# Expert stage with a weight ring of eight slots, scaled down products and the last sums behind the overflow jump

## The chip, the cores and the metric

The kernel runs on one core of a Trainium2 chip. The metric is the device time of one execution in microseconds (us). The engines are named as in the profile: PE is TensorE (PEld its weight loads), DVE is VectorE, ACT is ScalarE, POOL is GpSimd, SP is SyncE, which here only issues weight transfers.

## The reference

Two transformer blocks on 256 tokens of width 1024, all in float32. The first ends in a mixture of 32 experts, each token going to four of them; the second begins with a norm of the result. What matters here:

```python
def _moe(h, ...):
    logits = h @ router_w + router_b
    top_logit, top_e = lax.top_k(logits, 4)
    top_w = softmax(top_logit)
    ...
        gate = minimum(xe @ w_gate[e] + b_gate[e], 7.0)
        up = clip(xe @ w_up[e] + b_up[e], -7.0, 7.0)
        act = (up + 1) * (gate * sigmoid(1.702 * gate))
        return act @ w_down[e] + b_down[e]
    ...
    y = yb[dest] * sorted_w[:, None]
    return segment_sum(y, sorted_tok, num_segments=t)

# first block, end
x = x + g_m * moe(modulate(rmsnorm(x, norm_mlp), sh_m, sc_m))
# second block, start
h = rmsnorm(x, norm_mix_2); proj = h @ w_in_2
```

## The kernel before, in words

All weights stream through one ring of six slots (`RING`) of 2.097 MB; SP issues one transfer per block, in the order of use, each after a wait that TensorE has freed a block (`block_used`). The experts need 192 blocks: two halves each of w_gate, w_up and w_down for 32 experts, in eight groups of four (`EG`). Seven groups run in a hardware loop (`Fori`), the eighth is written out behind it. `expert_load` (L374) issues them; TensorE multiplies a half in `halves` (L1629), each 128x64 tokens by 512 columns.

A group on TensorE (`group_pe`): for each expert the gate product, the transpose of the previous expert's activation (L1651), the up product, then the previous expert's down product. In it lie the gather of the next group's tokens (L1617), the transpose of the slot weights (L1660), and two `combine` steps (L1677), which multiply the down results of a pair of experts by those slot weights, back to token order. VectorE adds the gate bias (L1115), clips (L1117), multiplies by the sigmoid (L1123), adds the up bias (L1125), and forms the activation (L1129); it fetches the next bias row by a shuffle (L1106). ScalarE makes the sigmoid (L638), and copies the down product from PSUM to `ypair` in two copies (`y_out`, L651 and L652). VectorE adds each of the four results of a combine from PSUM to the accumulator `acc` (L1141); two PSUM banks take them in turn, so a result waits until the one two before it has been read.

The down biases are multiplied by the token weights on TensorE at the start (L1718) and copied to `acc` by ScalarE (L685).

A token slot table holds 64 tokens per expert. If an expert has more, further passes run. The code of those passes is written out behind the first pass on every engine (`ov_passes`: a value is loaded, and a branch passes over it if it is 1). With these inputs the branch is always taken: 64 loads of w_gate are seen, those of one pass. After it VectorE multiplies `acc` by `g_moe` (L1188) and adds it to the residual `xres` (L1190), for each of two tiles of 128 tokens. ScalarE sums the squares of a tile (L606), VectorE forms the mean (L831), GpSimd the inverse root (L431), VectorE scales the tile (L1018), TensorE transposes it (L1573), ScalarE (L705) and VectorE (L1196) take the transposed halves out of PSUM. Then the projections of the second block begin (L1364, the helper of all ordinary products). GpSimd clears three tiles `Q2` for them (L447) as soon as `xres` is complete; ScalarE writes into the first of them from its first projection (L729).

Before the stage, the attention branches are merged (VectorE, `merged_done`, L1012), then come the output products (W_OUT, two blocks), the norm, the router products and the ranking on VectorE (L1050 to L1091). The arena area from column 13312 on holds `sig` and `prob`, last read before the merge ends.

## Time and profile before

| | us |
|---|---|
| median of 3 runs | 1884.38 (1884.05 to 1886.4) |
| the profiled execution | 1884.26 |
| its span, first to last instruction | 1882.5 |
| PE busy (share of the span) | 1706.3 (91%) |
| DVE busy | 454.0 (24%) |
| ACT busy | 306.4 (16%) |
| expert blocks issued, w_gate, w_up, w_down | 64 each, 2048 KB a block |

The profile is of one execution. Its page gives busy times and 40 slices of the span, 47 us each. The table of stretches gives the same for stretches one chooses, with the clock granted to TensorE as a share of 2.4 GHz, the mean share of the sixteen DMA engines, and GB/s. The chain of waits follows the work that ended last backwards, from each step to what released it. The list in order of time shows instructions merged into runs (x is their number). "issue" marks time in which an engine waited for nothing that the profile shows. A busy PE also counts the pipeline's filling.

### The profile page before, as it was taken

Reading aid. Unit: us, or ns where it says so; the run is one execution under the profiler, and the core shown is the slowest. Engines: PE = TensorE matmul, PEld = TensorE weight load, DVE = VectorE, ACT = ScalarE, POOL = GpSimd, SP = SyncE. Lnnn points to the kernel's source line nnn. Section 1 sums busy time; section 2 is a strip of 40 time slices with the busy share of each in tenths; the row PEclk is TensorE's granted clock in tenths of the full one; section 3 lists DMA queues with packets and bytes.
Section 4 is the critical chain, followed back from the end, with each engine's and each line's share of the span. In section 5 each row is a group of like instructions: output and inputs, shape, how many; then the busy total and the mean of one; then the engine's idle time right before and its main releaser. Section 6 shows DMA issues by size and latency. Waiting matters only on the chain.

```text
span 1882.5 us, 18274 instructions
## 1 busy us (share of the span) xinstructions
PE 1706.3 (91%) x7238; PEld 901.1 (48%) x7238; DVE 454.0 (24%) x928; ACT 306.4 (16%) x620; POOL 29.2 (2%) x30
## 2 busy tenths in 40 slices
PE   4999999899989898898988989875999999999998
PEld 1545686533233232332323323222767788588643
DVE  1342432232222222222222222224022221211001
ACT  2122450311010110110101101001242222000000
POOL 0110000000000000000000000001000000000000
PEclk9999999899999999999999999997999999989999
DMA  9776223499999999999999999998323233334410
GB/s 369 281 258 192 90 95 119 170 430 428 428 428 428 429 429 429 428 428 429 429 428 428 429 429 428 428 427 330 123 101 134 90 135 134 134 135 148 165 45 23
DMA packets 86888, 537.01 MB, mean 285 GB/s; under 512 B 4624, under 2 KB 5776, under 8 KB 62256
## 3 DMA queue, kind: packets, MB, share of 16 engines
q1 hardware_dynamic: 84736, 530.60, 69.7%
q10 hardware_dynamic: 2096, 5.64, 0.8%
q8 instruction: 38, 0.62, 0.1%
q14 instruction: 18, 0.15, 0.0%
HBM read 535.17 MB, written 1.05 MB: 285 GB/s over the span
## 4 chain that ended last, share of the span: by engine, by line
PE 73%; DMA 21%; DVE 3%; issue 2%; ACT 1%; SPq 1%; DVEq 0%; POOL 0%; POOLq 0%; ACTq 0%
PE ps L1364 33%; PE ps L1629 22%; DMA ring<-in_w_up 17%; PE ps L1925 5%; PE ps L1617 3%; PE ps L1677 3%; DMA ring<-in_w_down 3%; DMA ring<-in_w_ada 1%; PE ps L1377 1%; PE ps L1518 1%; PE ps L1651 1%; SPq L339 1%; DVE arena L1106 0%; PE ps L1470 0%; DVE arena L1018 0%
## 5 line engine op out<-in xcount | busy, mean ns | idle before, releaser
L1629 PE MATMUL ps<-ring,arena 128*64 128x512 f32 x3072 | 687.6, 598 | 79.7 <-DMA ring<-in_w_gate 33.3
L1629 PEld LDWEIGHTS ps<-ring,arena 128*64 128x64 f32 x3072 | 218.4, 137 | 524.6 <-issue 429.7
L1364 PE MATMUL ps<-arena,ring 128*128 128x256 f32 x1856 | 414.5, 383 | 2.8 <-ACT arena L705 2.5
L1364 PEld LDWEIGHTS ps<-arena,ring 128*128 128x128 f32 x1856 | 354.3, 192 | 62.8 <-issue 7.1
L1364 PE MATMUL ps<-ring,arena 128*128 128x512 f32 (+1 forms) x480 | 197.1, 566 | 4.6 <-issue 3.4
L1364 PEld LDWEIGHTS ps<-ring,arena 128*128 128x128 f32 x480 | 89.7, 190 | 103.6 <-issue 99.6
L1115 DVE TENSOR_TENSOR arena<-ps,arena 128x512 f32<-128x512 f32 x32 | 22.1, 692 | 383.5 <-PE ps L1629 383.5
L1925 PE MATMUL ps<-ring,arena 128*128 128x512 f32 x256 | 110.0, 592 | 0.0
L1677 PE MATMUL ps<-arena 128*128 128x512 f32 x128 | 68.2, 664 | 21.7 <-DVE arena L1141 20.4
L1125 DVE TENSOR_TENSOR arena<-ps,arena 128x512 f32<-128x512 f32 x32 | 22.1, 692 | 249.7 <-PE ps L1629 249.7
L1925 PEld LDWEIGHTS ps<-ring,arena 128*128 128x128 f32 x256 | 48.6, 190 | 60.8 <-issue 60.7
L643 ACT ACTIVATE arena<-ps 128x512 f32<-128x512 f32 x32 | 19.1, 597 | 347.7 <-PE ps L1651 347.7
L651 ACT ACTIVATE arena<-ps 64x512 f32<-64x512 f32 x32 | 18.9, 590 | 307.5 <-PE ps L1629 307.5
L1617 PE MATMUL ps<-arena 128*128 128x256 f32 x256 | 59.6, 393 | 3.9 <-DVE arena L1098 3.9
L1617 PEld LDWEIGHTS ps<-arena 128*128 128x128 f32 x256 | 49.6, 196 | 16.6 <-issue 5.7
L1141 DVE TENSOR_TENSOR arena<-ps,arena 128x512 f32<-128x512 f32 x64 | 43.6, 690 | 36.6 <-PE ps L1677 35.6
L431 POOL TENSOR_TENSOR stat<-stat 128x8 f32<-128x8 f32 (+3 forms) x22 | 23.6, 1074 | 1848.3 <-DVE stat L831 1848.3
L1377 PE MATMUL ps<-ring,router_weights 128*32 128x512 f32 x192 | 28.1, 710 | 25.6 <-DMA const<-in_const 17.3
L1677 PEld LDWEIGHTS ps<-arena 128*128 128x128 f32 x128 | 22.3, 200 | 58.3 <-DVE arena L1141 40.6
L606 ACT ACTIVATE arena<-xres 128x1024 f32<-128x1024 f32 x8 | 8.5, 1057 | 217.9 <-DVE xres L1336 109.4
L1106 DVE STREAM_SHUFFLE arena<-arena 128x1024 f32<-128x1024 f32 x33 | 42.9, 1299 | 0.3
L1329 DVE TENSOR_TENSOR arena<-arena 128x512 f32<-128x512 f32 x16 | 11.1, 692 | 104.1 <-ACT arena L821 104.1
(229 smaller groups left out, 915.0 us busy)
## 6 DMA issues: line engine op xcount, KB each, us to landing
ring<-in_w_up SPq DMA_DIRECT2D x72, 2048.0 KB, 21.3
ring<-in_w_down SPq DMA_DIRECT2D x72, 2048.0 KB, 25.5
ring<-in_w_gate SPq DMA_DIRECT2D x64, 2048.0 KB, 24.1
ring<-in_w_in SPq DMA_DIRECT2D x23, 2048.0 KB, 8.0
ring<-in_w_ada SPq DMA_DIRECT2D x12, 2048.0 KB, 16.0
ring<-in_w_out SPq DMA_DIRECT2D x4, 2048.0 KB, 7.8
ring<-in_w_branch SPq DMA_DIRECT2D x3, 2048.0 KB, 7.7
ring<-in_w_oa SPq DMA_DIRECT2D x2, 1024.0 KB, 11.6
```

What stands on the lines that cost most here:

```text
L431: pool.tensor_tensor(a, a, stat[:, 240:240 + a.shape[1]], ALU.pow).then_inc(sem("root_done"), 1)
L643: act.activation(actT, bank(3).rearrange("p (c f s) -> p c f s", c=4, f=2), ACT.Copy).then_inc(X["tr_read"], 1)
L1106: dve.stream_shuffle(bias, btab, [q] * 32)
L1115: dve.tensor_tensor(gbuf, bank(0), bias[:, 0:512], ALU.add).then_inc(X["gate_read"], 1)
L1125: dve.tensor_tensor(ubuf, bank(1), bias[:, 512:1024], ALU.add).then_inc(X["up_read"], 1)
L1141: dve.tensor_tensor(a, bank(6 + r % 2), a, ALU.add).then_inc(X["comb_read"], 1)
L1364: last = pe.matmul(dst, a, b, start=k == 0, stop=k == len(terms) - 1)
L1377: last = pe.matmul(bank(ada_bank(n))[32 * g:32 * g + 32, :], cs_t[:, 2 * g + c, :], w[:, 2 * g + c, :], start=c == 0, stop=c == 1)
L1617: last = pe.matmul(bank(4 + r % 2)[:, T * jj:T * jj + T], hperm[:, tt, j // 4, j % 4, :], S4[:, tt].rearrange("p e s -> p (e s)"), start=t ...
L1629: mm = pe.matmul(dst[CAP * g:CAP * g + CAP, :], stationary(half, c), w[:, c, 512 * g:512 * g + 512], start=half == 0 and c == 0, stop=half ...
L1677: pe.matmul(bank(6 + r % 2), WST[:, P * (2 * pr + tt):P * (2 * pr + tt) + P], ypair[:, pr, 512 * h:512 * h + 512], start=True, stop=True). ...
L1925: last = pe.matmul(bank(4 + 2 * tt + hh), hid[:, 4 * i + c, P * tt:P * tt + P], w[:, c, 512 * hh:512 * hh + 512], start=i == 0 and c == 0, ...
```

## The change

- Expert blocks go through eight slots: position k modulo 8 = 4 and 5 lie in the arena from column 13312 (two slots of 4096 columns), the others in the six of the ring. Each load now waits for the block eight before it (`MRING`). The first four expert blocks wait as before; the loads behind them wait besides for `merged_done`.
- The expert tiles in the arena move together to make room; `acc` goes away.
- The down products are taken out of PSUM by VectorE, multiplied by `g_moe` in the same instruction. The results of the combine steps are added straight into `xres`. The down biases are scaled by `g_moe` before their product, and the four results added to `xres` by VectorE.
- In the last group, the last down product's multiplication and the last four sums stand behind the overflow branch on VectorE (`finish`). The last combine on TensorE, ahead of its branch, writes to four banks and waits once, for the four sums of the combine before.
- GpSimd clears `Q2` after both tiles are scaled (`hx_xn`), no longer after the residual is complete.
- The second block's loads count on semaphores of their own; the first six take their slots from the last expert blocks.

```diff
+        def moe_ring(k):
+            s = k % MRING
+            return None if s in (4, 5) else (W_MOE + (s if s < 4 else s - 2)) % RING
+        def moe_block(k):
+            s = moe_ring(k)
+            a = ring[:, s * SLOT:(s + 1) * SLOT] if s is not None else area(13312 + SLOT * (k % MRING - 4), SLOT)
...
             with e.If(n > 1):
-                if before:
-                    before()
                 with e.Fori(1, n) as p:
+                    if before:
+                        before(p)
...
+                j = i - W_QKV2
+                if j >= RING:
+                    sp_.wait_ge(used2, j - RING + 1)
+                elif j >= 0:
+                    sp_.wait_ge(block_used, passes[0] * (GROUPS * GROUP_BLOCKS) + (W_MOE - MRING + (j if j < 4 else j + 2) + 1))
...
-                    sp_.wait_ge(X["used"], u * GROUP_BLOCKS + (X["before"] - RING + k + half + 1))
+                        sp_.wait_ge(X["used"], u * GROUP_BLOCKS + (X["before"] - MRING + k + half + 1))
...
+                expert_load(X, u0, 0, 0, 0, free=W_MOE - RING + 1 if first else None)
+                expert_load(X, u0, 0, 0, 1, free=W_MOE - RING + 3 if first else None)
+                if first:
+                    sp_.wait_ge(sem("merged_done"), 4)
...
-            pool.wait_ge(sem("x2_done"), 2)
+            pool.wait_ge(sem("hx_xn"), 2)
...
-            def y_out(X, u, q, last=False):
-                act.activation(y[r0:r0 + CAP, 0:512], bank(2)[0:CAP, :], ACT.Copy)
-                act.activation(y[r0:r0 + CAP, 512:1024], bank(2)[CAP:2 * CAP, :],
-                               ACT.Copy).then_inc(X["y_read"], 1)
+            def y_out(X, u, q, last=False):
+                dve.tensor_tensor(y[r0:r0 + CAP, 0:512], bank(2)[0:CAP, :], g_moe[0:CAP, 0:512], ALU.mult)
+                dve.tensor_tensor(y[r0:r0 + CAP, 512:1024], bank(2)[CAP:2 * CAP, :], g_moe[CAP:2 * CAP, 512:1024],
+                                  ALU.mult).then_inc(X["y_read"], 1)
...
+            def finish(X, it, u, final):
+                y_out(X, u, EG - 1, True)
+                for r in range(4):
+                    tt, h = r // 2, r % 2
+                    dve.wait_ge(X["comb_done"], it * 8 + (8 + r + 1))
+                    xx = xres[:, tt, 512 * h:512 * h + 512]
+                    add = dve.tensor_tensor(xx, bank((6, 7, 4, 5)[r]), xx, ALU.add)
+                    add.then_inc(sem("x2_done") if final else X["comb_read"], 1)
...
                 for q in range(1, EG):
                     gate_dve(X, u, q)
                     up_dve(X, it, u, q)
+                    y_out(X, u, q - 1)
                 if not last:
                     gate_dve(X, u, EG)
                 combine_dve(X, it, 0)
                 if not last:
+                    y_out(X, u, EG - 1)
                     up_dve(X, it, u, EG)
-                combine_dve(X, it, 1)
+                    combine_dve(X, it, 1)
...
+                if first:
+                    dve.tensor_tensor(bdown[0:N_EXP, :], bdown[0:N_EXP, :], g_moe[0:N_EXP, :],
+                                      ALU.mult).then_inc(sem("bd_read"), 1)
...
-            dve.drain()
-            for i in range(TT):
-                dve.tensor_tensor(acc[:, i, :], acc[:, i, :], g_moe[:, :], ALU.mult)
-                dve.drain()
-                dve.tensor_tensor(xres[:, i, :], xres[:, i, :], acc[:, i, :], ALU.add).then_inc(sem("x2_done"), 1)
+            n = ov_passes(dve, more_dve, lambda p: finish(X, p * GROUPS - 1, p * GROUPS - 1, False))
+            finish(X, n * GROUPS - 1, n * GROUPS - 1, True)
...
-            def combine(X, it, pr):
+            def combine(X, it, pr, last=False):
+                if last:
+                    pe.wait_ge(X["comb_read"], it * 8 + 5)
...
-                    pe.matmul(bank(6 + r % 2), WST[:, P * (2 * pr + tt):P * (2 * pr + tt) + P],
+                    pe.matmul(bank((6, 7, 4, 5)[r] if last else 6 + r % 2),
+                              WST[:, P * (2 * pr + tt):P * (2 * pr + tt) + P],
```

## Rows read from the trace of the kernel before

**Rows 1.** The page: part 2 (DMA share in tenths, 40 slices), part 4 by line.

```profile
DMA  9776223499999999999999999998323233334410
PE ps L1364 33%; PE ps L1629 22%; DMA ring<-in_w_up 17%; PE ps L1925 5%; PE ps L1617 3%; PE ps L1677 3%; DMA ring<-in_w_down 3%; DMA ring<-in_w_ada 1%; PE ps L1377 1%; PE ps L1518 1%; PE ps L1651 1%; SPq L339 1%; DVE arena L1106 0%; PE ps L1470 0%; DVE arena L1018 0%
```

**Rows 2.** Table of stretches, around and in the expert stage; columns in its first row.

```profile
core 0: us, PE busy (x) PEld busy (x) DVE busy (x) ACT busy (x) POOL busy (x), PEclk, DMA share, GB/s
310.00:325.00 15.00, 15.00 (x42) 7.08 (x41) 4.87 (x9) 2.22 (x6) 0.55 (x1) 1.00 0.02 7
340.00:360.00 20.00, 15.47 (x61) 12.37 (x62) 5.29 (x26) 7.38 (x11) 0.00 (x0) 0.67 0.00 0
412.00:1277.00 865.00, 765.38 (x3320) 279.57 (x3320) 218.03 (x339) 93.18 (x155) 0.00 (x0) 0.99 1.01 428
1277.00:1310.00 33.00, 13.80 (x52) 6.13 (x48) 15.17 (x16) 5.42 (x14) 6.33 (x5) 0.73 1.04 383
```

**Rows 3.** In order of time, SP's issues: start, length to the last one's end.

```profile
287.57 16.49 SPq L374 DMA_DIRECT2D ring<-in_w_up  x2
325.39 6.46 SPq L374 DMA_DIRECT2D ring<-in_w_gate  x2
362.48 3.77 SPq L374 DMA_DIRECT2D ring<-in_w_up  x2
```

**Rows 4.** The waits of TensorE: total us, times, longest.

```profile
PE ps L1629 <- DMA ring<-in_w_gate: 33.3, 29, 1.3
```

**Rows 5.** Groups of instructions in the stage: busy, mean ns, idle before.

```profile
L651 ACT ACTIVATE arena<-ps 64x512 f32<-64x512 f32 x32 | 18.9, 590 | 307.5 <-PE ps L1629 307.5
L1115 DVE TENSOR_TENSOR arena<-ps,arena 128x512 f32<-128x512 f32 x32 | 22.1, 692 | 383.5 <-PE ps L1629 383.5
```

**Rows 6.** The chain that ended last, 1262 to 1312 us: start, us, what.

```profile
1268.10 3.65 PE ps L1629 x16
...
1275.97 7.04 PE ps L1629 x32
...
1284.28 3.91 PE ps L1677 x8
...
1289.20 5.68 issue
...
1302.30 5.70 DVE arena L1018
...
1308.05 1.13 PE ps L1573 x4
```

**Rows 7.** In order of time, 1262 to 1312 us: start, us, engine, line, idle before.

```profile
1276.01 0.69 DVE L1141 TENSOR_TENSOR arena<-ps,arena 128x512 f32<-128x512 f32 x1 [0.17 <-PE ps L1677]
...
1284.30 0.38 ACTq L699 DMA_DIRECT2D g_attn<-in_norm_final  x1
...
1285.44 0.69 DVE L1141 TENSOR_TENSOR arena<-ps,arena 128x512 f32<-128x512 f32 x1 [8.74 <-PE ps L1677]
...
1299.89 0.15 DVE L831 TENSOR_SCALAR stat<-stat 128x1 f32<-128x1 f32 x1
...
1301.57 1.97 PE L1573 MATMUL ps<-const,arena 128*128 128x128 f32 x8 [13.40 <-DVE arena L1018]
...
1302.15 5.30 POOL L447 MEMSET arena<- 128x2048 f32 x3
...
1311.28 16.28 PE L1364 MATMUL ps<-arena,ring 128*128 128x256 f32 x64 [1.26 <-ACT arena L705]
```

**Rows 8.** DMA queues: instruction packets, MB, share: 1291 to 1292, then 1292 to 1293.

```profile
q8 instruction: 1, 0.02, 6.8%
...
q14 instruction: 1, 0.01, 2.5%
```

**Rows 9.** Table of stretches, around TensorE's idle time; columns as in rows 2.

```profile
1290.00:1295.00 5.00, 0.00 (x0) 0.00 (x0) 0.00 (x0) 0.00 (x0) 0.00 (x0) 0.69 1.05 385
1315.00:1320.00 5.00, 5.00 (x23) 4.32 (x22) 0.00 (x0) 0.00 (x0) 0.00 (x0) 0.92 0.00 0
```

More of the change, by code:

```diff
@@ L277, in two_blocks, with moe_loaded, moe_loads_before @@
         loaded = [sem(f"block_loaded{s}") for s in range(RING)]
-        X1 = {n: sem("x_" + n) for n in (
+        X = {n: sem("x_" + n) for n in (
             "gate_read", "gate_min", "up_read", "sig_done", "act_done", "tr_done", "tr_read", "y_read",
             "comb_done", "comb_read", "s4_ready", "ws4_ready", "gather_done", "gather_read")}
-        X2 = dict(X1)
-        X1["used"], X1["loaded"], X1["before"], X1["slot"] = block_used, loaded, W_MOE, W_MOE
-        X2["used"] = sem("more_block_used")
-        X2["loaded"] = [sem(f"more_block_loaded{i}") for i in range(RING)]
-        X2["before"], X2["slot"] = RING, 0
+        X["used"], X["before"] = block_used, W_MOE
+        MRING = 8
+        def moe_ring(k):
[4 more added lines that the diff above has]
+            a = ring[:, s * SLOT:(s + 1) * SLOT] if s is not None else area(13312 + SLOT * (k % MRING - 4), SLOT)
+            return a.rearrange("p (c n) -> p c n", c=4)
+        def moe_loaded(k):
+            s = moe_ring(k)
+            return sem(f"extra_loaded{k % MRING - 4}") if s is None else loaded[s]
+        def moe_loads_before(k):
+            s = moe_ring(k)
+            return 0 if s is None else len(range(s, W_MOE, RING))
+        loaded2 = [sem(f"block2_loaded{s}") for s in range(RING)]
+        used2 = sem("block2_used")
         block = ctx.enter_context(nc.Block())
@@ L1357, in tell_used @@
                 if owed[0]:
-                    first.then_inc(block_used, 1)
+                    first.then_inc(used_now[0], 1)
                 owed[0] = False
@@ L1623, in halves @@
                 for half in range(2):
-                    i = X["slot"] + weight_block(q, m, last) + half
-                    pe.wait_ge(X["loaded"][i % RING], u * (16 * GROUP_BLOCKS // RING) + 16 * (i // RING + 1))
-                    w = w4_view(i)
+                    b = weight_block(q, m, last) + half
+                    pe.wait_ge(moe_loaded(b), u * (16 * GROUP_BLOCKS // MRING) + 16 * (moe_loads_before(b) + b // MRING + 1))
+                    w = moe_block(b)
                     for c in range(4):
@@ L1703, in group_pe @@
                     up(X, it, u, EG)
-                combine(X, it, 1)
+                combine(X, it, 1, last)
             def slot_bias_transpose():
@@ L1931, in _ @@
                 if i < 7:
-                    last.then_inc(block_used, 1)
+                    last.then_inc(used2, 1)
 def launch_arrays(inp):
```

147 lines of the change are left out of this document (74 added, 73 removed).

## The prediction

> **What bounds the kernel now.** I read the chain that ended last first, by line [rows 1]. A third of it is ordinary TensorE work in the attention parts and the second block (L1364), nearly all the rest is the expert stage: matmuls of L1629 and waits for the transfers of w_up and w_down. Then the table of stretches [rows 2]. In the expert stage, 412 to 1277 us, the sixteen DMA engines are busy the whole time (share 1.01, 428 GB/s) while TensorE is busy for 765 of 865 us: the stage is bound by its weight transfers, 192 blocks of 2.097 MB. Such a block takes 2.097 MB / 428 GB/s = 4.90 us. TensorE's own waits for weights are short and many (29 waits for w_gate, 33.3 us) [rows 4]: it uses every block as it lands, with the ring nearly empty. Before the stage the same engines stand still: share 0.02 in 310 to 325, 0.00 in 340 to 360 [rows 2]. The issue queue shows why [rows 3]: six blocks are out at 331.9 us (two w_gate at 325.39, the second some 6 us later), and the seventh needs a slot that TensorE frees only at 362.48. Last, the end of the stage, step by step [rows 6, 7]: after the last down product (ends 1283.0) there are 28.25 us to the first projection of the next block (1311.28), in which TensorE does little. In them stand a gap of 5.68 us on VectorE in which no visible thing is waited for, at the place where it jumps over the code of the overflow passes, and a normalisation of 5.70 us for tile 1, where the same instruction took 0.75 us for tile 0.
>
> **Ring of eight.** The blocks of group positions 4 and 5 of every eight go to two arena slots. The wait of the first two (merged_done 4 and the 22nd and 23rd freed block) is over when the pair of [rows 3] at 287.57 has gone out (304.1), because merged_done is counted by VectorE before the output products begin. They move in 304 to 325, where the engines stand nearly still. The two after them take the issue times of today's blocks 4 and 5, 325.39 and about 331.5, and land before 340. So at 362.48 eight blocks are there, not six. Nothing later is issued at another condition: each transfer still waits for a block that TensorE frees, and until 412 TensorE runs without a wait for weights, so it frees them at today's times. From then on the engines are busy throughout, so the landing of block n depends on how many blocks are still to move: two fewer, 2 x 4.90 = 9.8 us earlier. Lower bound of this gain: 0 (if something else paces the stage); upper bound 9.8. I take 9.8, since the share is 1.01 from 412 to 1277 and 1.04 from there to 1310 [rows 2]. The last down product waits for the second half of down product 2 (TensorE restarts on it at 1268.10), not for its own blocks, so its end moves with the transfers from 1283.0 to 1273.2.
>
> **Down products read by VectorE.** Two copies of 0.59 us on ScalarE per expert (L651, its twin L652) become two multiplications on VectorE. The nearest row is the 128x512 sum with one PSUM operand, 0.69 us (L1115) [rows 5]: 1.45 us with gaps, 32 times, 46 us more VectorE work spread over 915 us. It hides behind TensorE's products of 7.1 us per matrix: the 32 instructions of L1115 alone waited 383.5 us for TensorE [rows 5]. Behind the waiting multiplication VectorE has the next gate sum (TensorE waits for that one two products later), whose product ends 7 us after the down product. If that cover were gone, TensorE would lengthen by at most 46 us, and it has 100 us of idle time in [rows 2]. Price 0. The same holds for the scaling of the down biases (32 partitions, once, before TensorE's first gate product ends) and for the four bias sums that go from ScalarE to VectorE (4 x 0.69 us, before the up product of expert 0 ends).
>
> **The end of the stage.** I count from the end of the last down product. Today: 1.25 us for the two ScalarE copies, 3.9 us of combine (starts 1284.28), VectorE's last sum, the gap, two multiplications and two sums over 128x1024, the normalisation, 28.25 in all.
> Changed: VectorE makes its jump after the first four sums of the last group, not after the last four. Those end at 1276.70 today (the last starts at 1276.01 [rows 7]), 6.3 us before the down product ends. The jump costs 5.68 plus some 0.4 us around it, so it is just covered. Then 1.5 us (two multiplications) to the combine, which needs no sums in between as it has four banks, 3.9 us, ends at 5.4. The sums into the residual start 1.16 us after each result (1284.28 to 1285.44) and are paced by it at 0.86: the last ends at 5.95. ScalarE squares tile 0 from 4.2, tile 1 from 6.0. From the mean (L831, 1299.89) to TensorE's transpose (1301.57) are 1.7 us [rows 7]: tile 0 is ready at 7.7, tile 1, 1.5 us behind, at 9.2. The scaled products make the two multiplications and the separate sums (4 x 1.2 us) fall away.
> Now what is late next. TensorE also has the overflow code to skip, and it makes its jump after the combine, at 5.4. Today that is hidden behind 13.4 us of idling. Its price has no row of its own, but the instruction queues have two: a packet of 16 KB at 1291 to 1292 (q8) and one of 8 KB at 1292 to 1293 (q14) [rows 8], both during VectorE's gap, and VectorE goes on at 1294.9. So two engines fetch, and one is TensorE (the queue with the larger packets: no other engine has nearly as long a program to pass over). Its packet comes 3.4 us after its combine ends, VectorE's 3.7 us after its gap begins. Bounds: 0, as on ScalarE, which issues its next transfer at 1284.30, 0.07 us after its last copy [rows 7]; and 13.4, the idle time that covers it. I take VectorE's 5.7. TensorE then starts at 11.1, 1.9 us after tile 1 is ready, does the eight transposes of tile 0 in 1.97, and the projections start 3.2 us after the second eight begin (1308.05 to 1311.28): 11.1 + 2.0 + 3.2 = 16.3 us instead of 28.25. Gain 12.0.
> The Trainium skill, "Runtime: NRT & Kernel Launch", section Instruction fetch mechanics, says that a taken branch whose target lies outside the pages held forces a fetch before execution goes on; it speaks against leaving TensorE's jump where it is. The two packets agree. By it alone TensorE waits and the gain of this part is 12.0; were the jump free, 15.3.
>
> **Later clearing.** GpSimd's three memsets (1302.15, 5.30 us) and tile 1's normalisation (1302.30, 5.70 us) begin and end together [rows 6, 7]: the normalisation waited them out. They now start when both tiles are done, at 9.2, and end at 14.6. ScalarE first needs the cleared tile some 9.4 us after the projections start, at 25. The 4.9 us are inside the 12.0 above. Unknown is whether VectorE's reads of transposed tiles (from PSUM) are held as well: no row. If they are, those of tile 0, due at 13.1, wait until 14.6, and the projections move by 0.7 at most; bounds 0 and 0.7, I take 0.
> On this the Trainium skill, "GPSIMD Engine Reference", section Specifications, says that GpSimd's SBUF interface is contended by Vector instructions in a two-port mode or with two SBUF inputs. The reads in question have one input, in PSUM; by it the price is 0, by the held row 0.7.
>
> **TensorE's clock.** It fell to its lower level (1.2 GHz) in 1290 to 1295, after TensorE had stood still since 1288.2, and was back at the upper (2.4 GHz) within 1315 to 1320, mean 0.92 [rows 9], so about 4.5 us into the projections; half of that, 2.3 us, was lost. The idle stretch is now 5.7 us, so I let it fall again and take 0, with a gain of 2.3 as bound.
>
> **Sum.** 9.8 + 12.0 = 21.8 us. All after 1311 is one dense TensorE chain that moves as a whole: its transfers take at most four tenths of the engines [rows 1]. Four of its blocks can be issued before the last down product, the others right behind. Span 1882.5 - 21.8 = 1860.7; the profiled execution took 1884.26, 1.8 us more than its span, and stands 0.1 under the median of 1884.38. Forecast 1862.5.
>
> **Rivals.**
> TensorE's jump is hidden: it may prefetch further than VectorE. Then the transposes start at 7.7, the projections at 12.9, gain 9.8 + 15.3 = 25.1: 1859.2. For it: ScalarE's free jump. Against: the 16 KB packet after the jump. 0.13.
> VectorE's jump is no longer covered: 6.1 us stand against 6.3, and the fetch now queues behind 16 KB pieces of expert weights. At twice 5.7 the multiplications start 5.5 us late and everything behind them: 1868.0; at half of that surcharge 1865. 0.14.
> The lead of two blocks is lost, by a stage that TensorE or a queue paces: only the 12.0 stay, 1872.3. Against: share 1.01. 0.06.
> Slower: the arena slots. 48 of the 192 blocks now land beside the buffers that the engines write. The other level of the engines in this trace is 383 GB/s (1277 to 1310, share 1.04, columns of the next matrices) [rows 2], 5.48 us a block. Were it theirs in these slots, 48 x 0.58 = 28 us are lost: 1862.5 + 28 = 1890. It decides from 0.45 us a block, 21.8 / 48. Against: the rate held 428 on average while all four engines worked in the arena. 0.03.
>
> **How the numbers follow.** The forecast with its own spread of 2 us (clock, memset) has 0.62; the rest, 0.02, is an effect below what can be told. The range 1857.5 to 1868 takes the forecast, the hidden jump with the clock's gain and the uncovered jump, and leaves out the lost lead and the arena: 0.87 to 0.89. A change within 0.2%, 3.8 us, is about what a measurement of this kernel can't tell from none. Faster 0.95 (0.62 + 0.13 + 0.14 + 0.06), same 0.02, slower 0.03.
>
> **What would show it.** Two transfers right behind 303.7; eight out before 340; the landing of the last expert block 9.8 us earlier. On VectorE a gap of about 6 us between the fourth and the multiplication of the last down product. On TensorE a gap of 5 to 6 us after the last combine while normalised tiles lie ready. The normalisation of tile 1 at 0.75 us. Wrong I would be with a DMA share under 1 in the stage, or a first multiplication that begins well after the last down product ended.

## The result and the profile after

| | before | changed |
|---|---|---|
| median, us | 1884.81 (4 runs) | 1858.54 (4 runs, 1857.39 to 1859.68) |
| ratio | | 0.9855, interval 0.9842 to 0.9868 |
| the profiled execution, its span | 1884.26, 1882.5 | 1857.39, 1855.0 |

By the ratio the change takes 27.3 us off (0.9855 of 1884.4 is 1857.1); the two medians of the table lie 26.3 apart, the two spans 27.5. The forecast was 21.8, with a range of 1857.5 to 1868, so the time by the ratio lies just below the range. Line numbers shift: `halves` is now L1669, the combine L1720, the ordinary products L1404, the transposes L1613, the normalisation L1025 (mean L838), the multiplications of the down product L1147 and L1148, the sums into the residual L1157 and, behind the jump, L1166.

The page of the changed kernel: part 1, the DMA share of part 2, and part 4 by line.

```profile
PE 1704.2 (92%) x7238; PEld 901.3 (49%) x7238; DVE 492.9 (27%) x993; ACT 266.5 (14%) x552; POOL 29.2 (2%) x30
...
DMA  9766225499999999999999999999333234334310
...
PE ps L1404 33%; PE ps L1669 19%; DMA ring<-in_w_up 11%; DMA ring<-in_w_gate 9%; PE ps L1969 6%; PE ps L1657 3%; PE ps L1720 2%; DMA arena<-in_w_down 2%; DMA arena<-in_w_up 2%; DMA ring<-in_w_ada 1%; PE ps L1417 1%; PE ps L1558 1%; SPq L361 0%; PE ps L1510 0%; PE ps L1533 0%
```

TensorE is busy for nearly the same time as before (1704.2 against 1706.3); what went is its idling. Some 39 us of work moved from ScalarE to VectorE. The row of nines, the stage, is as unbroken as in [rows 1], and the seventh slice (278 to 325 us) rose from 3 to 5. The list in order of time, SP's issues of expert blocks before and at the start of the stage (beside [rows 3]):

```profile
287.29 16.49 SPq L398 DMA_DIRECT2D ring<-in_w_up  x2
304.19 1.14 SPq L398 DMA_DIRECT2D arena<-in_w_gate  x2
324.92 6.48 SPq L398 DMA_DIRECT2D ring<-in_w_up  x2
362.35 3.76 SPq L398 DMA_DIRECT2D ring<-in_w_down  x2
```

The two arena blocks go out at 304.19, and the block issued at 362.35 is the ninth. The table of stretches (columns as in [rows 2]):

```profile
310.00:325.00 15.00, 15.00 (x42) 7.10 (x41) 4.87 (x10) 2.52 (x6) 0.55 (x1) 1.00 0.66 282
340.00:360.00 20.00, 15.45 (x61) 12.21 (x63) 6.50 (x27) 7.65 (x11) 0.00 (x0) 0.67 0.00 0
412.00:1267.00 855.00, 766.09 (x3332) 280.31 (x3332) 260.15 (x399) 57.69 (x95) 0.00 (x0) 0.99 1.01 429
```

The engines that stood at 0.02 in 310 to 325 now work at 0.66, and the stage is still paced by its transfers, at 1.01. Then the end of the stage, from the chain that ended last:

```profile
1255.46 3.65 PE ps L1669 x16
...
1263.33 7.04 PE ps L1669 x32
...
1271.84 3.71 PE ps L1720 x8
1275.56 0.02 issue
1275.58 0.69 DVE xres L1166
...
1277.82 1.20 issue
1279.02 2.83 PE ps L1613 x12
...
1283.96 16.19 PE ps L1404 x64
```

The projections are those of the next block. With these rows the time can be put down by stretch. The first expert product begins at 358.79 before and 358.52 after.

| us | before | after | difference | forecast |
|---|---|---|---|---|
| first expert product to TensorE's last wait for weights | 909.31 | 896.94 | -12.4 | -9.8 |
| that wait's end to the end of the last down product | 14.9 | 14.9 | 0 | 0 |
| end of the last down product to the next block's projections | 28.29 | 13.61 | -14.7 | -12.0 |
| the rest, to the end | 571.22 | 571.04 | -0.2 | 0 |

With 0.3 us ahead of the stage these are the 27.5 us of the spans, but for rounding. Both terms of the forecast are there, and each was larger: by 2.6 and by 2.7 us. The experiments ask what each term is made of.

### The profile page after: what moved, and what is told of

It is laid out like the page before. It is cut to its first block, busy times and chain, and to the rows that moved or that the text cites. A ratio compares the mean times of both kernels' runs of the same rounds, so it can differ in the third digit from the quotient of the medians.

```text
span 1855.0 us, 18279 instructions
## 1 busy us (share of the span) xinstructions
PE 1704.2 (92%) x7238; PEld 901.3 (49%) x7238; DVE 492.9 (27%) x993; ACT 266.5 (14%) x552; POOL 29.2 (2%) x30
## 3 DMA queue, kind: packets, MB, share of 16 engines
HBM read 535.17 MB, written 1.05 MB: 289 GB/s over the span
## 4 chain that ended last, share of the span: by engine, by line
PE 70%; DMA 26%; DVE 1%; issue 1%; ACT 1%; SPq 0%; DVEq 0%; POOL 0%; POOLq 0%; ACTq 0%
PE ps L1404 33%; PE ps L1669 19%; DMA ring<-in_w_up 11%; DMA ring<-in_w_gate 9%; PE ps L1969 6%; PE ps L1657 3%; PE ps L1720 2%; DMA arena<-in_w_down 2%; DMA arena<-in_w_up 2%; DMA ring<-in_w_ada 1%; PE ps L1417 1%; PE ps L1558 1%; SPq L361 0%; PE ps L1510 0%; PE ps L1533 0%
## 5 line engine op out<-in xcount | busy, mean ns | idle before, releaser
L1669 PE MATMUL ps<-ring,arena 128*64 128x512 f32 x2304 | 512.1, 595 | 56.7 <-DMA ring<-in_w_gate 28.8
L1404 PE MATMUL ps<-arena,ring 128*128 128x256 f32 x1856 | 414.3, 383 | 2.8 <-ACT arena L712 2.5
L1404 PEld LDWEIGHTS ps<-arena,ring 128*128 128x128 f32 x1856 | 354.3, 192 | 62.7 <-issue 7.1
L1669 PEld LDWEIGHTS ps<-ring,arena 128*64 128x64 f32 x2304 | 164.1, 137 | 385.7 <-issue 317.2
L1404 PE MATMUL ps<-ring,arena 128*128 128x512 f32 (+1 forms) x480 | 197.1, 566 | 4.6 <-issue 3.4
L1669 PE MATMUL ps<-arena 128*64 128x512 f32 x768 | 174.3, 603 | 13.1 <-DMA arena<-in_w_up 10.7
L1404 PEld LDWEIGHTS ps<-ring,arena 128*128 128x128 f32 x480 | 89.7, 190 | 103.6 <-issue 99.6
L1669 PEld LDWEIGHTS ps<-arena 128*64 128x64 f32 x768 | 53.4, 139 | 127.1 <-issue 108.3
L1720 PE MATMUL ps<-arena 128*128 128x512 f32 x128 | 69.0, 667 | 21.1 <-DVE xres L1157 19.6
L1122 DVE TENSOR_TENSOR arena<-ps,arena 128x512 f32<-128x512 f32 x32 | 22.1, 692 | 210.4 <-PE ps L1669 210.4
L1147 DVE TENSOR_TENSOR arena<-ps,g_moe 64x512 f32<-64x512 f32 x32 | 21.9, 683 | 189.4 <-PE ps L1669 189.4
L1132 DVE TENSOR_TENSOR arena<-ps,arena 128x512 f32<-128x512 f32 x32 | 22.1, 692 | 186.7 <-PE ps L1669 186.7
L1720 PEld LDWEIGHTS ps<-arena 128*128 128x128 f32 x128 | 23.2, 201 | 57.7 <-DVE xres L1157 38.3
L1157 DVE TENSOR_TENSOR xres<-ps,xres 128x512 f32<-128x512 f32 x60 | 40.7, 690 | 20.1 <-PE ps L1720 18.3
## 6 DMA issues: line engine op xcount, KB each, us to landing
arena<-in_w_up SPq DMA_DIRECT2D x16, 2048.0 KB, 28.3
```

Source lines behind the costliest of these rows:

```text
L1122: dve.tensor_tensor(gbuf, bank(0), bias[:, 0:512], ALU.add).then_inc(X["gate_read"], 1)
L1132: dve.tensor_tensor(ubuf, bank(1), bias[:, 512:1024], ALU.add).then_inc(X["up_read"], 1)
L1147: dve.tensor_tensor(y[r0:r0 + CAP, 0:512], bank(2)[0:CAP, :], g_moe[0:CAP, 0:512], ALU.mult)
L1157: dve.tensor_tensor(xx, bank(6 + r % 2), xx, ALU.add).then_inc(X["comb_read"], 1)
L1404: last = pe.matmul(dst, a, b, start=k == 0, stop=k == len(terms) - 1)
L1669: mm = pe.matmul(dst[CAP * g:CAP * g + CAP, :], stationary(half, c), w[:, c, 512 * g:512 * g + 512], start=half == 0 and c == 0, stop=half ...
```

## The experiments

A ratio is always to the kernel before on the same chip. The medians of one kernel differ by up to 3 us from one set of runs to the next; where less is at stake I go by the stretches of the trace, and say so. "In the stage" means from the first expert product to TensorE's last wait for weights, "at its end" from the end of the last down product to the projections.

### The changed kernel once more, and without its lead

> The changed kernel once more, beside the others of this group. Its profiled execution moved 300.78 MB in 450 to 1150 us, the kernel before 299.93 MB in the same 700 us, 0.28% less, which over the 905 us of the expert stage is 2.6 us. If that belongs to the kernel (the rate theory), this run shows 300.6 to 301.0 MB again and 27 us less than before; if it varies from execution to execution (the chance theory), the megabytes or the time fall between the two, and the gain is 24.5 to 27.5.

Measured: 1855.70 us, ratio 0.9852 (0.9838 to 0.9865); 897.11 us in the stage, 13.64 at its end. It repeats within 0.2 us by stretch. Seven traces whose stage runs the same transfers (these two, e3 to e7) lie between 896.94 and 898.66 us in the stage, so a difference under 2 us between two single stages is not read below.

Undo the two slots alone:

```diff
-        MRING = 8
+        MRING = 6
-            return None if s in (4, 5) else (W_MOE + (s if s < 4 else s - 2)) % RING
+            return (W_MOE + s) % RING
...
-(W_MOE - MRING + (j if j < 4 else j + 2) + 1))
+(W_MOE - MRING + j + 1))
```

> The changed kernel with six slots, all in the ring, nothing else altered. The lead theory (two blocks less ready when TensorE begins, the rate is that of any ring) expects the landing of the last expert blocks 2 x 4.88 = 9.8 us later than with eight slots, 1868.3 us. The rate theory (a deeper queue moves 0.28% more) expects that and 2.6 us more, 12.4 later, 1870.9, with 299.9 MB in 450 to 1150. If neither depth nor lead counted, 1858.5.

Measured: 1868.90 us, ratio 0.992 (0.9907 to 0.9934). The stage is back at 909.43 us, its end stays at 13.34. So the two parts are separate, and the two slots are worth some 12 us of stage (12.3 against the repeat of the changed kernel, 13.2 by the medians), not 9.8.

Keep the slots, but hold back all blocks from the fifth on until TensorE has freed the first expert block:

```diff
                 if first:
                     sp_.wait_ge(sem("merged_done"), 4)
+                    sp_.wait_ge(block_used, W_MOE + 1)
```

> Eight slots, but the transfers from the fifth expert block on wait until TensorE has used the first expert block (362.4 us), so four blocks fewer lie ready at that moment. The lead theory expects 4 x 4.88 = 19.5 us more than the changed kernel, 1878.0. If depth alone counted (the lead being without worth), nothing is lost. The rate theory expects the eight-slot megabytes (300.8 in 450 to 1150) also here, the chance theory no relation.

Measured: 1875.30 us, ratio 0.9951 (0.9937 to 0.9964), 19.6 us above the changed kernel; 916.02 us in the stage, 19.0 more. The last wait for weights ends at 1272.92, only 17.4 us later, but this execution also began its first expert product 1.6 us earlier, at 356.90; against e5 and e6, which began at 357.24 and 357.06 and took 898.01 and 898.66 us, the stage is 17.4 to 18.0 longer. Four blocks of 4.9 us were held back, 19.5 in all: a lead is worth about the transfer time of its blocks. Without the early start eight slots are no better than six (916.02 against 909.43): what counts is blocks moved while the DMA engines would stand still. (300.76 MB in 450 to 1150 us, as in the changed kernel, so its quicker rate is not a matter of the lead.)

### Why the two slots give 12.4 us

Six slots again, but two of them, positions 4 and 5 of six, in the arena:

```diff
-        MRING = 8
+        MRING = 6
...
-(W_MOE - MRING + (j if j < 4 else j + 2) + 1))
+(W_MOE - MRING + min(j, 3) + 1))
```

> Six slots again, but four in the ring and two in the arena; the next block's first four loads take the ring slots, the next two the free ones. With six slots in the ring 299.89 MB moved in 450 to 1150 us, with eight, two of them in the arena, 300.76 (also with the late start). If the depth of the queue makes the 0.29%, this run moves 299.9 MB and takes the 1869 us of six slots; if the place of the slots makes it, 300.7 MB and some 2.5 us less, 1866.4.

Measured: 1865.95 us, ratio 0.9892 (0.9871 to 0.9914), 906.04 us in the stage: 3.4 less than with six slots in the ring, with no more lead than those. So the place of the slots has a value of its own. It shows in the totals of 450 to 1150 us, where the DMA engines never pause. The view of the DMA queues, in the order before, changed kernel, e1, r1:

```profile
DMA packets 20594, 299.93 MB, mean 428 GB/s; under 512 B 2288, under 2 KB 2288, under 8 KB 2288
```
```profile
DMA packets 20646, 300.78 MB, mean 430 GB/s; under 512 B 2288, under 2 KB 2288, under 8 KB 2288
```
```profile
DMA packets 20590, 299.89 MB, mean 428 GB/s; under 512 B 2286, under 2 KB 2286, under 8 KB 2286
```
```profile
DMA packets 20665, 301.06 MB, mean 430 GB/s; under 512 B 2290, under 2 KB 2290, under 8 KB 2290
```

The more blocks go to the arena, the more is moved in the same 700 us: none 299.9 MB, a quarter 300.8, a third 301.1. Over all eighteen traces the total is steadier than the time: with the same placement it repeats within 0.1 MB. What differs is the address. A slot is 16,384 bytes in each partition. By the order and sizes of the tiles (the profile shows no addresses) the ring begins at byte 16,512 of a partition, 128 above a multiple of 256, and with it each of its slots; the two arena slots begin at 195,840 and 212,224, both multiples of 256. The theory: a transfer whose pieces begin at a multiple of 256 bytes in SBUF goes quicker. Its rivals: something else of the arena's place, or of the order of use. The test moves the ring, with no other edit:

```diff
+        modT = ctx.enter_context(nc.sbuf_tensor("modT", [P, 48, 2], F32))
         ring = sb("ring", RING * SLOT)
...
-        modT = ctx.enter_context(nc.sbuf_tensor("modT", [P, 48, 2], F32))
```

modT has 384 bytes; the ring then begins at a multiple of 512, the arena slots 128 bytes above one.

> The changed kernel with modT allocated ahead of the ring: the six ring slots then begin at a multiple of 512 bytes in SBUF (before: 128 above one), the two arena slots 128 above one (before: 256 above). The excess of the bytes moved in 450 to 1150 us over the 299.9 MB of six ring slots was 0.88 MB with a quarter of the blocks in the arena and 1.16 MB with a third, so some 3.5 MB for all of them. If the start address modulo 512 makes it, the ring slots are now the quick ones: 299.9 + 0.75 x 3.5 = 302.5 MB, 5 us less than the changed kernel, or more. If it is the region of SBUF (the arena lies higher), 300.8 MB and no difference.

Measured: 1850.91 us, ratio 0.9827 (0.9809 to 0.9844), 894.39 us in the stage. The three placements beside it:

> As the run before, and the arena moved by 128 bytes less so that its slots begin at a multiple of 512 as well. By the address theory all blocks are quick: 303.4 MB in 450 to 1150, 8 us less than the changed kernel (0.88%/300 of 905 us). By the region theory nothing.

Measured: 1851.21 us, ratio 0.9828 (0.9809 to 0.9846), 895.46 us in the stage.

> The changed kernel with 128 bytes ahead of the ring: ring slots at 256 above a multiple of 512, arena slots at 384. By the address theory with 256 as the unit 302.5 MB, as in the run with the ring at 512; if only a multiple of 512 counted, the arena slots at 256 above would not have been quick before. By the region theory 300.8.

Measured: 1853.66 us, ratio 0.9841 (0.9822 to 0.986), 894.07 us.

> The changed kernel with all eight slots at 256 above a multiple of 512. With the ring at 128 the two arena slots at 256 brought an excess of 0.88 MB, a quarter of 3.5; were the excess of a slot a matter of its own address alone, all eight would move 303.4 MB, 8 us less than the changed kernel. The runs with the ring at 512 or 256 all moved 301.9 whatever the arena slots' place, which speaks for a ceiling there: then 301.9 MB and 1852 us.

Measured: 1850.56 us, ratio 0.9814 (0.9795 to 0.9832), 894.46 us. In s2 and s4 the arena slots lie 128 above a multiple of 256, in s3 and s5 they are aligned as well. All four moved the same, 301.89 to 301.91 MB: a multiple of 512 gives nothing over 256, and neither do the aligned arena slots.

The same on the kernel before, where nothing else of the change is in play. b1 puts 128 bytes ahead of the ring (the edit shown), b2 moves modT there, b3 moves `forget_weights` (256 bytes) ahead of it, so that the ring shifts and stays 128 above a multiple of 256:

```diff
+        pad = sb("pad", 32)
         ring = sb("ring", RING * SLOT)
```

> The kernel before, with 128 bytes of SBUF put ahead of its ring of six slots (ring at 256 above a multiple of 512, before 128), nothing else. If the place of the slots alone makes the transfers' rate, it moves 301.9 MB in 450 to 1150 us instead of 299.93, as the changed kernel with its ring there did; 0.66% of 905 us, 6 us less: 1878.9. If the quicker rate needs the eight slots or the rest of the change, 299.9 MB and 1884.8.

> The kernel before with modT allocated ahead of the ring (ring at a multiple of 512). The same alternatives as the run beside it: 301.9 MB and 1878.9 us if the place makes the rate, 299.9 and 1884.8 if not.

> The kernel before with the forget weights allocated ahead of the ring: ring slots at 384 bytes above a multiple of 512, so 128 above a multiple of 256, as at first, but 256 bytes further on. If a start at a multiple of 256 bytes makes the quicker transfers, this one is slow: 299.9 MB in 450 to 1150 us, 1884.8 us. If any move away from the old place did, 301.9 MB and 1877.9.

Measured: b1 1877.74 us, ratio 0.9957 (0.9942 to 0.9971), 903.57 us in the stage; b2 1877.91, ratio 0.9954 (0.9939 to 0.9969), 903.61; b3 1884.61, ratio 1.0 (0.9988 to 1.0012), 909.31 us in the stage, as before the change. 128 unused bytes ahead of the ring take 5.7 us off the stage of the kernel before and 7 off its median; a shift that keeps the remainder takes nothing. The view of the DMA queues, 450 to 1150, of b2, b3 and s2:

```profile
DMA packets 20732, 301.93 MB, mean 431 GB/s; under 512 B 2304, under 2 KB 2304, under 8 KB 2304
```
```profile
DMA packets 20592, 299.88 MB, mean 428 GB/s; under 512 B 2289, under 2 KB 2289, under 8 KB 2289
```
```profile
DMA packets 20728, 301.89 MB, mean 431 GB/s; under 512 B 2302, under 2 KB 2302, under 8 KB 2302
```

b1 moved 301.84 MB. So shifts of 128 and 384 bytes make the ring quick, and shifts of 0 and 256 leave it slow, whatever the absolute address is. These edits move the other tiles behind the ring too, and with them what the engines read and write; r1 moves no tile, only which slots the blocks use, and its rate rose all the same. So the theory stands for the two remainders tried, 0 and 128; no other was run.

Now the lead can be taken by itself: with an aligned ring the stage lasts 903.6 us with six slots (b1, b2) and 894.1 to 895.5, on average 894.6, with eight (s2 to s5). That is 9.0 us for two blocks of 4.86 us (2.097 MB at 431.3 GB/s), where 9.7 were due. The other 3 us of the 12.4 are the address: 0.85 MB more in 700 us are 2.6 us in the 905 of the stage, an estimate from the totals above.

### What VectorE's new work costs

The down products are copied by ScalarE again, at its old places. The scaling by g_moe is left out, which the expectation says too.

```diff
+                act.activation(y[r0:r0 + CAP, 0:512], bank(2)[0:CAP, :], ACT.Copy)
+                act.activation(y[r0:r0 + CAP, 512:1024], bank(2)[CAP:2 * CAP, :],
+                               ACT.Copy).then_inc(X["y_read"], 1)
```

> The changed kernel with the down products copied from PSUM by ScalarE again, two copies of 0.59 us per expert, without the multiplication by g_moe (which this kernel leaves out). The cover theory of the prediction says that VectorE's 1.45 us per expert hide behind TensorE's products: the landing of the last expert blocks and the time stay, save 0.2 us at the last down product (1.25 instead of 1.45 us), 1855.5 on the scale of the changed kernel's 1855.7. If VectorE's extra work held TensorE up in the stage, the time falls by more than 1 us and TensorE's idle time before its products shrinks.

Measured: 1857.78 us, ratio 0.9855 (0.9834 to 0.9876); 897.20 us in the stage, where the changed kernel has 896.94 and 897.11, and 13.57 at its end. The two times lie within the spread of one kernel: the 64 multiplications cost nothing that can be told. In the changed kernel VectorE still waits for TensorE ahead of them; two groups of the page:

```profile
L1122 DVE TENSOR_TENSOR arena<-ps,arena 128x512 f32<-128x512 f32 x32 | 22.1, 692 | 210.4 <-PE ps L1669 210.4
L1147 DVE TENSOR_TENSOR arena<-ps,g_moe 64x512 f32<-64x512 f32 x32 | 21.9, 683 | 189.4 <-PE ps L1669 189.4
```

The wait of 383.5 us of [rows 5] is now split over two instructions, and none of it is gone.

### The end of the stage, piece by piece

The last sums ahead of VectorE's jump, as it was before:

```diff
-            n = ov_passes(dve, more_dve, lambda p: finish(X, p * GROUPS - 1, p * GROUPS - 1, False))
-            finish(X, n * GROUPS - 1, n * GROUPS - 1, True)
+            finish(X, GROUPS - 1, GROUPS - 1, True)
+            ov_passes(dve, more_dve)
```

> The last down multiplication and the last four sums ahead of VectorE's overflow branch (the extra passes themselves are then left incomplete; they are not entered here). If the branch costs VectorE the 6.1 us of the kernel before wherever it stands, the mean of tile 0 is formed at 1282.4 instead of 1276.19, tile 1's transposes begin at 1285.6 instead of 1280.9, and the kernel loses 4.7 us, with a gap of 6 us in front of the mean. If the cost belonged to the two large multiplications or the drain that stood there, the gap is under 1 us and the loss nil.

Measured: 1861.32 us, ratio 0.9871 (0.9853 to 0.9889); 18.5 us from the end of the last down product to the projections, 4.9 more than in the changed kernel. The list in order of time, VectorE's first instruction behind the jump:

```profile
1283.79 0.15 DVE L838 TENSOR_SCALAR stat<-stat 128x1 f32<-128x1 f32 x1 [5.99 <-issue]
```

The gap is 5.99 us here. In the same list the kernel before has 6.12, of which the chain of [rows 6] shows 5.68. In the changed kernel the jump lies under the last down product. The first 64 projections took 14.05 us in e4 (TensorE's clock was back at the upper level by 1290), against 16.19 in the changed kernel, so part of the 4.9 came back there.

The last combine with two banks and its waits, as in the other combines (VectorE's sums read the same two banks, an edit not shown):

```diff
                     if not last:
                         pe.wait_ge(X["comb_read"], it * 8 + (1 if 4 * pr + r < 2 else 4 * pr + r))
+                    elif r >= 2:
+                        pe.wait_ge(sem("x2_done"), r - 1)
-                    pe.matmul(bank((6, 7, 4, 5)[r] if last else 6 + r % 2),
+                    pe.matmul(bank(6 + r % 2),
```

> The last combine in two banks again, its third and fourth product waiting for VectorE's first and second sum (the extra passes are left incomplete). The run-ahead theory says that TensorE's sequencer reaches its branch as soon as nothing before it waits, some 3 us before the last combine product ends, so that the fetch overlaps the products (gap 3.5 us). With waits in the combine it reaches the branch only after the second sum, at about 1274.6; the first transposes then begin 2 us later (about 1281, gap 5 to 5.5 us), as do the projections. The rival, that the fetch begins when the combine ends and was merely quicker than VectorE's, expects the gap of 3.5 us and the same time.

Measured: 1860.09 us, ratio 0.9865 (0.984 to 0.989); 16.4 us at the end of the stage, 2.8 more than the changed kernel. The medians alone don't tell the two apart; the rows do. The list in order of time around TensorE's jump, first of the changed kernel, then of e6 (where the combine is L1722):

```profile
1271.84 3.70 PE L1720 MATMUL ps<-arena 128*128 128x512 f32 x8 [1.50 <-DVE arena L1148]
...
1279.02 3.67 PE L1613 MATMUL ps<-const,arena 128*128 128x128 f32 x16 [3.48 <-issue]
```
```profile
1272.11 3.89 PE L1722 MATMUL ps<-arena 128*128 128x512 f32 x8 [1.50 <-DVE arena L1148]
...
1282.05 3.68 PE L1613 MATMUL ps<-const,arena 128*128 128x128 f32 x16 [6.05 <-issue]
```

And the packet of TensorE's instruction queue, in the view of the DMA queues, of 1276 to 1277 in the changed kernel and of 1279 to 1280 in e6:

```profile
q8 instruction: 1, 0.02, 6.8%
```
```profile
q8 instruction: 1, 0.02, 6.8%
```

The combine lasts the same to 0.2 us. In windows of a tenth of a microsecond the packet of 16 KB begins between 1276.4 and 1276.5 in the changed kernel and between 1279.4 and 1279.5 in e6: 4.6 and 7.3 us after the combine's start, and TensorE goes on 2.6 us later both times. That the fetch begins when the combine has ended is thereby out: it would have come at the same distance in both. What fits is that without waits TensorE's sequencer runs ahead of the engine and stands at the branch before the last products are done. The trace has no record of the sequencer there, so how far ahead it is stays an inference from the packet. The Trainium skill, "Runtime: NRT & Kernel Launch", section Instruction fetch mechanics, says that a taken branch out of the pages held forces a fetch before execution goes on. The two packets agree; what decides the price here is how early the fetch can begin.

TensorE without its jump (its overflow passes are not there at all):

```diff
-            ov_passes(pe, lambda p: pass_pe(X, p * GROUPS, p * GROUPS, False))
```

> TensorE's program without the code of the overflow passes, hence without its branch; with these inputs they are never entered, and the kernel leaves them out for other inputs. In the changed kernel TensorE stands still for 3.48 us between the last combine and the first transpose, while tile 0 is ready 1.2 us before it, tile 1 at 1279.35, 1.5 us before its transposes. If the fetch behind the branch is what it waits for, the first transposes start right after tile 0 (gap 2.3 us instead of 3.48) and the second right after tile 1, 1.2 to 1.5 us saved: 1857.1. If something else holds it, the gap stays 3.5 us and the time 1858.5.

Measured: 1855.82 us, ratio 0.9853 (0.984 to 0.9867), as the changed kernel on the same chip (1855.70). Its trace, the list in order of time:

```profile
1277.65 1.09 PE L1613 MATMUL ps<-const,arena 128*128 128x128 f32 x8 [2.32 <-DVE arena L1025]
...
1281.55 14.05 PE L1404 MATMUL ps<-arena,ring 128*128 128x256 f32 x64 [1.26 <-ACT arena L712]
```

The transposes start when tile 0 is ready, the gap ahead of them is put down to VectorE, no longer to issue, and no packet of 16 KB comes before them: it was TensorE's. The projections start 11.4 us after the last down product, 2.2 earlier than in the changed kernel. But the clock has a part in that: it did not fall in this execution, the transposes ran at its upper level (1.09 us for eight, where all sixteen took 3.67 in the changed kernel), and so did the projections (14.05 us for 16.19). s2 keeps the jump and kept the upper clock too, and has 11.75 us. So at the upper clock 0.3 us are left of TensorE's jump, and the medians show no gain from its removal. In the changed kernel TensorE stood 1.20 us longer than tile 0 needed (the issue row of the chain at 1277.82), which bounds its price there.

GpSimd clears at its old place:

```diff
-            pool.wait_ge(sem("hx_xn"), 2)
+            pool.wait_ge(sem("x2_done"), 4)
```

> The changed kernel with GpSimd's clearing waiting for the residual again, not for the scaled tiles. It can begin when the second root is done, about 1278.5 us, when the scaling of tile 1 begins (1278.59). If the three memsets hold that instruction, as before the change, it takes 5.3 to 5.7 us instead of 0.75, tile 1's transposes begin at about 1284 instead of 1280.9, and the kernel loses 3.1 to 3.2 us (4.9 less what TensorE's jump hides). If the earlier 5.70 us came from something else, nothing changes.

Measured: 1862.99 us, ratio 0.9873 (0.9852 to 0.9894); 15.5 us at the end of the stage, 1.9 more than in the changed kernel, where 3.1 to 3.2 were expected. The time grew by more than that; in the profiled execution TensorE's clock was still at 0.50 in 1285 to 1290, and the first 64 projections took 16.79 us and the second 64 16.55, against 16.19 and 14.06. The list in order of time of e3:

```profile
1279.41 5.83 POOL L473 MEMSET arena<- 128x2048 f32 x3
1279.56 3.94 DVE L1025 TENSOR_SCALAR arena<-xres,stat 128x1024 f32<-128x1024 f32 x1 [0.72 <-POOL stat L457]
...
1285.57 1.13 DVE L1231 TENSOR_SCALAR arena<-ps,vec 128x128 f32<-128x128 f32 x4 [1.04 <-PE ps L1613]
```

and of the changed kernel:

```profile
1278.59 0.75 DVE L1025 TENSOR_SCALAR arena<-xres,stat 128x1024 f32<-128x1024 f32 x1 [0.72 <-POOL stat L457]
...
1279.40 5.29 POOL L473 MEMSET arena<- 128x2048 f32 x3 [0.91 <-DVE arena L1025]
...
1281.02 1.13 DVE L1231 TENSOR_SCALAR arena<-ps,vec 128x128 f32<-128x128 f32 x4 [1.68 <-PE ps L1613]
```

The scaling of tile 1 takes 3.94 us beside the memsets and 0.75 without them. It was 5.70 in [rows 7], and both values come back in the kernel before: b2 has 5.69, b1 and b3 have 3.94. The list in order of time of b3:

```profile
1303.91 5.84 POOL L447 MEMSET arena<- 128x2048 f32 x3
1304.06 3.94 DVE L1018 TENSOR_SCALAR arena<-xres,stat 128x1024 f32<-128x1024 f32 x1 [0.72 <-POOL stat L431]
```

One memset takes 1.8 us. Where the scaling took 5.7 us it ended 0.5 us after the third; where it took 3.94 it ended 0.5 us after the second, and the third was 0.54 us longer. So the scaling waits for whole memsets, for three or for two, from one execution to the next, and the early clearing costs 3.2 or 4.9 us in this instruction. VectorE's reads from PSUM take 1.13 us for four, beside the memsets (1281.02) as after them (1285.57): they are not held, which the trace of before left open. The Trainium skill, "GPSIMD Engine Reference", section Specifications, puts the contention for SBUF on VectorE's instructions in a two-port mode or with two SBUF inputs; these reads have one input, in PSUM, and the trace agrees.

## Why the prediction was right and where it was not

**The lead: right in mechanism, nearly right in size.** Two blocks leave at 304.19, behind the pair of 287.29, the engines move them while they would stand still, and the whole stage shifts by them. e1 and e2 show it from both sides. Its 9.8 us were 9.0 when the ring is aligned on both sides (b1, b2 against s2 to s5).

**The arena slots: wrong in sign.** The bounds of the gain, 0 and 9.8, left no room above, and the rival on the arena gave it only a price, of up to 28 us. The step that failed is the bound: it took the rate of a block to be the same wherever it lands, or worse. The blocks in the arena are quicker, which r1 shows without any lead, and the remainder of the start address modulo 256 is the cause, which b1 to b3 show. It accounts for some 3 us of the 12.4; with the lead at 9.0 in place of 9.8 the term came out 2.6 too small. No row of before could have told it, since all of its expert blocks land at one remainder; the addresses could have raised the question.

**VectorE's work: right, price 0** (e7).

**VectorE's jump: right.** Covered, as forecast; uncovered in e4 it lengthens the end by 4.9 us.

**TensorE's jump: half right.** It is there and its packet too, but "it makes its jump after the combine, at 5.4", failed. By the forecast's own count from the end of the last down product:

| us after the end of the last down product | forecast | changed | e6 |
|---|---|---|---|
| combine ends | 5.4 | 5.2 | 5.4 |
| tile 0 ready | 7.7 | 7.5 | 7.7 |
| tile 1 ready | 9.2 | 9.0 | 9.2 |
| TensorE goes on | 11.1 | 8.7 | 11.4 |
| projections start | 16.3 | 13.6 | 16.4 |

The column of e6 is the forecast to 0.3 us: with waits in the combine the sequencer cannot run ahead, and the count holds. Four banks and no waits, which I took only as a shorter combine, hide 2.6 us of the jump and shorten the combine by 0.2. The forecast read the price from the packet's place in before (3.4 us after the combine ended); that combine had waits too, and counted from its start, 1284.28, the packet began 7.3 us later in both, before and e6.

**Later clearing: right.** Tile 1 at 0.75 us, the PSUM reads free. Inside the end of the stage it was worth 1.9 us in e3, where the scaling waited for two memsets only. The 5.70 us of [rows 7], which the forecast took for the price, was the dearer of two cases: in b3 the end of the kernel before lasted 26.6 us, not 28.3. So 1.7 of the 14.7 us in the table above, and of the forecast's 12.0 alike, hang on which case the profiled execution of the kernel before happened to show.

**The clock: right for the profiled execution.** It fell, as before; in s2, s4 and e5 it did not. The table of stretches of the changed kernel:

```profile
1275.00:1280.00 5.00, 1.52 (x7) 0.98 (x6) 2.73 (x6) 1.89 (x4) 1.68 (x3) 0.81 1.05 385
1280.00:1285.00 5.00, 3.73 (x16) 3.18 (x15) 2.25 (x8) 2.29 (x8) 4.70 (x3) 0.50 1.05 385
1285.00:1290.00 5.00, 5.00 (x17) 4.13 (x16) 0.00 (x0) 0.00 (x0) 0.00 (x0) 0.67 1.05 387
```

0.50 is the lower of its two levels, 1.2 GHz, after TensorE had stood still from 1275.5 to 1279.0. The first projections took 16.19 us, as the 16.28 of [rows 7].

The sum of the two failed sizes, 2.6 on the transfers (12.4 against 9.8) and 2.7 on the jump, with 0.5 us ahead of the stage and behind it, is what lies between 21.8 and the 27.5 of the spans.

**A version quicker than both kernels.** s5, the changed kernel with every slot at a multiple of 256 bytes, ran in 1850.56 us, ratio 0.9814 (0.9795 to 0.9832); s2 and s3 lie within 0.7 us of it, s4 3.1 above it, with ratios of 0.9827 to 0.9841. By the trace of s2 against the changed kernel: 2.6 us of stage, 1.9 at its end (1.7 of it the transposes) and 2.1 in the first projections. The last two come with the clock, which did not fall there (1.00 in 1280 to 1285) and did in s5 (0.50). Of the three, only the stage is shown to come from the address, by the four runs together rather than by this one pair.

## What to carry to other kernels

In a stage that its transfers bound, slots are worth the blocks that they let move while the engines would stand still, and the start address of the slots belongs to the design as much as their number: count the bytes of a long steady stretch and compare slots with different remainders. Where an engine passes over code, put work that waits for others behind the jump, and keep waits out of the last instructions ahead of it, so that the sequencer reaches the branch while the engine still computes.

## What the runs showed of the hardware

- Transfers of 16 KB in each partition into SBUF move 428.4 GB/s (299.9 MB in 700 us) where the pieces begin 128 bytes above a multiple of 256, and 431.3 GB/s (301.9 MB) where they begin at one. The gain is not in proportion to the blocks aligned: a quarter brings 0.9 MB and a third 1.2, at which rate all would bring 3.5, but three quarters (s2, s4) and all (s3, s5) bring the same 2.0. What caps it stays open.
- The Trainium skill, "DMA: Bandwidth & Descriptors", section How a descriptor splits into AXI transactions, tells of a cost of this kind for what a descriptor reads: one that does not start at a multiple of 256 bytes needs a further transaction. For a piece of 16 KB that is 65 for 64, an estimate of 1.6%. The runs show 0.67%, on the side that is written. The cause behind it was not tested further.
- While the next block's matrices follow (1275 to 1285) the rate was 385 GB/s in the changed kernel, 404 to 406 in s2 and 403 to 404 in s5, and in 1290 to 1295 it was 403 in b1 and b2, where the kernel before moved 385. So the lower level of [rows 2] depends on the address too.
- The clock of TensorE does not fall and return at the same point in each execution. The start of the first expert product varied from 357.06 (e6) to 362.11 us (e7), with no edit ahead of it; in e7 the granted clock was 0.87 in 325 to 340. The first 64 projections took 14.05 us or between 15.5 and 16.8. These differences are of the size by which runs of one kernel lie apart.
- A VectorE scaling of 128x1024 that meets GpSimd's memsets of 128x2048 (1.8 us each) takes 3.94 or 5.69 us in place of 0.75 (e3, b1, b3; before, b2).
- A branch over code costs VectorE about 6 us (gaps of 6.12 us in before, 5.99 in e4, 5.81 in b1) with the DMA engines at a share of 1.04 to 1.05. No run measured it with these engines idle.
